# Weight split and convolution taps moved from GpSimd to VectorE in a two-block transformer kernel

## What is computed

```
h    = rms_norm(x) * w
proj = h @ w_in                        # 4128 columns, twice; 6176 columns once
# second block, of the projection's columns:
q,k,v (512 columns each)               # neighbourhood attention, with a norm over heads of 64
c    = short_conv(proj[..., 1024:2560])  # y[t] = w0*x[t-1] + w1*x[t] + w2*x[t+1], per channel
c    = silu(c); q,k parts: l2 norm over heads of 64, rotary embedding for the 1024 latent tokens
o    = gated delta rule over chunks of 64 tokens
```

## Time and profile before

| | |
|---|---|
| median of 3 runs | 4703.82 us (4698.98 to 4707.6) |
| the profiled execution, its own time | 4698.29 us |
| its span | 4696.4 us |
| PE busy | 3419.8 us, 73% |
| DVE busy | 2311.5 us, 49% |
| ACT busy | 1230.9 us, 26% |
| POOL busy | 860.2 us, 18% |
| granted TensorE clock, mean | 0.840 |

### The profile page before, as it was taken

The page is one execution under the profiler, slowest core; times in us unless marked ns, Lnnn a source line. Parts: engine busy times, 40 slices in busy tenths (PEclk is TensorE's granted clock), DMA queues, the critical chain, the costliest instruction groups (busy, mean ns, idle before and its releaser), DMA issues. The chain is left out here.

```text
span 4696.4 us, 75209 instructions
## 1 busy us (share of the span) xinstructions
PE 3419.8 (73%) x32108; PEld 2802.8 (60%) x32108; DVE 2311.5 (49%) x3831; ACT 1230.9 (26%) x2110; POOL 860.2 (18%) x724
## 2 busy tenths in 40 slices
PE   4997555567568995563767489977776779887688
PEld 4997454145238994453443279977765658776333
DVE  3111887377461116885766511056746844554333
ACT  2111332034231113330433211022234422221322
POOL 1221342110102122432001021132311012221100
PEclk9998656789779996655998689988887878999788
DMA  3222000540433221003013222155333121121411
GB/s 126 95 96 70 14 21 25 184 113 23 130 103 100 95 85 39 21 14 117 22 56 133 90 98 79 65 177 175 123 120 102 37 56 49 40 49 52 155 73 47
DMA packets 260142, 383.91 MB, mean 82 GB/s; under 512 B 46495, under 2 KB 192727, under 8 KB 258396
## 3 DMA queue, kind: packets, MB, share of 16 engines
q1 hardware_dynamic: 154618, 253.55, 17.2%
q10 hardware_dynamic: 105190, 125.55, 7.8%
HBM read 262.05 MB, written 123.13 MB: 82 GB/s over the span
## 5 line engine op out<-in xcount | busy, mean ns | idle before, releaser
L356 PE MATMUL psum<-proj_w_low,h_high 128*128 128x344 f32 (+1 forms) x2080 | 691.5, 332 | 55.0 <-POOL proj_w_low L341 55.0
L356 PE MATMUL psum<-proj_w_high,h_high 128*128 128x344 f32 (+1 forms) x2080 | 689.9, 332 | 0.0
L356 PE MATMUL psum<-proj_w_high,h_low 128*128 128x344 f32 (+1 forms) x2080 | 689.6, 332 | 0.0
L380 DVE COPY proj_y<-psum 128x344 f32<-128x344 f32 (+1 forms) x130 | 70.8, 545 | 964.8 <-PE psum L356 964.8
L356 PEld LDWEIGHTS psum<-proj_w_low,h_high 128*128 128x128 f32 x2080 | 392.0, 188 | 64.2 <-issue 56.1
L356 PEld LDWEIGHTS psum<-proj_w_high,h_high 128*128 128x128 f32 x2080 | 392.1, 188 | 8.1
L356 PEld LDWEIGHTS psum<-proj_w_high,h_low 128*128 128x128 f32 x2080 | 391.9, 188 | 8.2
L341 POOL TENSOR_TENSOR proj_w_low<-proj_raw,proj_cut 128x2752 fp32r<-128x2752 f32 (+1 forms) x31 | 203.0, 6549 | 1019.9 <-DVE proj_cut L371 1019.9
L403 ACT ACTIVATE proj_y<-psum 128x344 f32<-128x344 f32 (+1 forms) x130 | 61.9, 476 | 766.6 <-PE psum L356 766.6
L1256 PE MATMUL psum<-merge_wo,merge_yt 128*128 128x512 f32 x512 | 226.8, 601 | 13.5 <-ACT merge_yt L1201 10.0
L356 PE MATMUL psum<-proj_rest_w_low,h_high 128*128 128x304 f32 x640 | 199.5, 312 | 23.9 <-POOL proj_rest_w_low L341 23.2
(11 more groups left out here) (401 smaller groups left out, 7208.8 us busy)
## 6 DMA issues: line engine op xcount, KB each, us to landing
proj_raw<-in_w_in SPq DMA_DIRECT2D x24, 1376.0 KB, 6.8
proj<-proj_y ACTq DMA_DIRECT2D x192, 172.0 KB, 1.9
delta_x<-dn_qkv SPq DMA_DIRECT2D x40, 384.0 KB, 5.1
proj<-proj_y ACTq DMA_DIRECT2D x68, 224.0 KB, 1.9
dn_prep_x<-proj SPq DMA_DIRECT2D x54, 256.0 KB, 3.6
proj_raw<-in_w_in SPq DMA_DIRECT2D x7, 1792.0 KB, 7.4
norm_x<-x_stream SPq DMA_DIRECT2D x24, 512.0 KB, 3.3
modulate_w<-in_mod_w SPq DMA_DIRECT2D x6, 2048.0 KB, 9.0
```

What stands on the lines that cost most here:

```text
L356: last = PE.matmul(self.ps[:, j % 4, 0:self.width], hp[:, kt, tokens], wp[:, c % 2, kt, :], start=kt == 0 and n == 0, stop=kt == KT - 1 an ...
L380: V.tensor_copy(self.y[:, j % 4, :], self.ps[:, j % 4, 0:self.width]).then_inc(*self.copied[1].inc())
```

## The change

The low parts of the weights are written by DVE instead of POOL, right behind the cut. All three products of the convolution are on DVE, in one stream with the sums; the second sum moves from place 4u+2 to 4u+1, and ACT's first silu instructions from 4u+2.6 to 4u+1.6. Project gets `act_share`: with 1 the copies alternate as before, with 2 ACT makes them all; only `proj2_rest` gets 2. In NaPrepare, PE's transposes move from 3n+1.5 to 3n+2.2 and ACT's copy from 3n+2 to 3n+2.9. POOL keeps its other work in other stages.

```diff
@@ Project.__init__
-        self.high, self.low = self.event("act", "high", n_cols), self.event("pool", "low", n_cols)
+        self.high, self.low = self.event("act", "high", n_cols), self.event("dve", "low", n_cols)
         self.product = self.event("pe", "product", n)
-        self.copied = self.event("act", "copied0", n // 2), self.event("dve", "copied1", n // 2)
+        self.on_act = [j % 2 < act_share for j in range(n)]
+        self.copied = [self.event(e, f"copied_{e}", self.on_act.count(on)) for e, on in (("act", True), ("dve", False))]
@@ Project
-    def pool(self):
-        G = self.nc.gpsimd
-        for c in range(len(self.groups)):
-            yield self.start(c) + 2.7
-            G.wait_ge(*self.cutoff(c))
-            if c >= 2:
-                G.wait_ge(*self.product(self.first[c - 1] - 1))
-            G.tensor_tensor(self.wl[:, c % 2], self.raw[:], self.cut[:], ALU.subtract).then_inc(*self.low.inc())
+    def copy_of(self, j):
+        on = self.on_act[j]
+        return self.copied[0 if on else 1](self.on_act[:j].count(on))
@@ Project.pe
-                PE.wait_ge(*self.copied[j % 2](j // 2 - 2))
+                PE.wait_ge(*self.copy_of(j - 4))
@@ Project.dve_split
             V.tensor_scalar(self.cut[:].bitcast(U32), self.raw[:].bitcast(U32), HIGH, None, ALU.bitwise_and).then_inc(*self.cutoff.inc())
+            yield self.start(c) + 2.7
+            V.wait_ge(*self.cutoff(c))
+            if c >= 2:
+                V.wait_ge(*self.product(self.first[c - 1] - 1))
+            V.tensor_tensor(self.wl[:, c % 2], self.raw[:], self.cut[:], ALU.subtract).then_inc(*self.low.inc())
@@ Project.dve_copies
-        for j in range(1, self.items, 2):
+        for j in range(self.items):
+            if self.on_act[j]:
+                continue
@@ Project.act_copies
-        for j in range(0, self.items, 2):
+        for j in range(self.items):
+            if not self.on_act[j]:
+                continue
@@ NaPrepare.pe
-            yield 3 * n + 1.5
+            yield 3 * n + 2.2
@@ NaPrepare.act
-            yield 3 * n + 2
+            yield 3 * n + 2.9
@@ DeltaPrepare
-    def pool_unit(self, u):
-        G, s = self.nc.gpsimd, u % 2
-        yield 0
-        G.wait_ge(*self.loaded[s](self.loads[u]))
-        if u >= 2:
-            G.wait_ge(*self.done(u - 2))
-        G.tensor_tensor(self.tmp[:, s], *self.tap(u, 0), ALU.mult).then_inc(*self.tap0.inc())
-        yield 1.3
-        G.wait_ge(*self.tap_added(u))
-        G.tensor_tensor(self.tmp[:, s], *self.tap(u, 2), ALU.mult).then_inc(*self.tap2.inc())
@@ DeltaPrepare.dve_unit
-        c(V.tensor_tensor(y, *self.tap(u, 1), ALU.mult))
+        V.tensor_tensor(y, *self.tap(u, 1), ALU.mult)
+        c(V.tensor_tensor(tmp, *self.tap(u, 0), ALU.mult))
+        c(V.tensor_tensor(y, y, tmp, ALU.add))
         yield 1
-        V.wait_ge(*self.tap0(u))
-        V.tensor_tensor(y, y, tmp, ALU.add).then_inc(*self.tap_added.inc())
-        yield 2
-        V.wait_ge(*self.tap_added(u))
-        V.wait_ge(*self.tap2(u))
+        c(V.tensor_tensor(tmp, *self.tap(u, 2), ALU.mult))
         V.tensor_tensor(y, y, tmp, ALU.add).then_inc(*self.conv.inc())
@@ DeltaPrepare.act_unit
-        yield 2.6
+        yield 1.6
@@ build
-        rest = Project(k, "proj2_rest", above, h, [late] * 10, w2, 304, p2, 3136, row2)
+        rest = Project(k, "proj2_rest", above, h, [late] * 10, w2, 304, p2, 3136, row2, 2)
```

More of the change, by code:

```diff
@@ L301, with __init__ @@
 class Project(Stage):
-    def __init__(self, k, name, bottom, h_t, groups, w, width, dst, col0=0, row_of=lambda t: t * P):
+    def __init__(self, k, name, bottom, h_t, groups, w, width, dst, col0=0, row_of=lambda t: t * P, act_share=1):
         super().__init__(k, name, bottom)
@@ L408, in act_keeps @@
             yield j + 1.3
-            S.wait_ge(*self.copied[j % 2](j // 2))
+            S.wait_ge(*self.copy_of(j))
             row, first = self.row_of(t), self.col0 + c * self.width
@@ L1751, in __init__ @@
         self.stores = [sum(stores[u % 2:u + 1:2]) - 1 for u in range(n)]
-        self.tap0, self.tap2 = sig("pool", "tap0", n), sig("pool", "tap2", n)
-        self.tap_added, self.conv, self.logs = (sig("dve", x, n) for x in ("tap_added", "conv", "logs"))
+        self.conv, self.logs = (sig("dve", x, n) for x in ("conv", "logs"))
         self.logged, self.sigmoid = (sig("act", x, n) for x in ("logged", "sigmoid"))
@@ L1786, in tap @@
         return self.x[:, u % 2, d], self.w[:, d, self.C * part:self.C * part + self.C]
-    def pool(self):
-        self.nc.gpsimd.wait_ge(*self.consts(0))
-        yield from self.each(self.pool_unit)
-    def pool_unit(self, u):
-        G, s = self.nc.gpsimd, u % 2
-        yield 0
-        G.wait_ge(*self.loaded[s](self.loads[u]))
-        if u >= 2:
-            G.wait_ge(*self.done(u - 2))
-        G.tensor_tensor(self.tmp[:, s], *self.tap(u, 0), ALU.mult).then_inc(*self.tap0.inc())
-        yield 1.3
-        G.wait_ge(*self.tap_added(u))
-        G.tensor_tensor(self.tmp[:, s], *self.tap(u, 2), ALU.mult).then_inc(*self.tap2.inc())
     def dve(self):
```

## The result

Over 20 runs each on the same chip the kernel before took 4713.3 us (median) and the changed one 4687.6 us: ratio 0.9945, 95% interval 0.9929 to 0.996. That is 26 us less, between 19 and 33. The profiled execution of the changed kernel took 4685.6 us with a span of 4683.7, against 4698.3 and 4696.4 for the one that the earlier trace rows come from.

What follows compares the result with a forecast made beforehand. PE was taken to bound the lone projections, DVE the shared stage, a DVE-ACT-PE chain the attention stage. -12.2 - 32.1 - 5.1 + 0.9 = -48.5 took the median from 4703.8 to 4655.3 us; range 4622 to 4684.

Steps and rivals of the forecast that it cites:

- Term 1, the starts: Starts of all four projections: low parts on DVE at 1.07 ns an element bring the first matmuls sooner, -12.2 us.
- rival D: Low parts on DVE much slower than 1.07 ns an element, so starts gain nothing and shared stage loses 21; 4688, chance 0.03.
- Term 2, the shared stage: Shared stage: DVE's waits for POOL go, -32.1 us, and NaPrepare's later transposes give -5.1.
- I keep these whole: Shared stage: DVE's waits for a store and the rotation table, 57.4 us, stay unchanged; 64.5 idle in all.
- Rival A: PE becomes the bound of the shared stage and all 63.6 us of its wait go; 4622, chance 0.13.
- I allow 0 to +10: Shared stage: copies queued behind ACT's waits for DVE could hold PE a few us; counted as 0.
- The shift of NaPrepare's places: Shared stage: transposes 1.54 places later pay once, at the end, with fewer items left behind them, -5.1 us.
- signs of being wrong: PE newly waiting for ACT's copies, DVE's L1814 (now L1804) idle above 80 us, or PE never waiting for L1428.
- Term 3, the attention stage: Attention stage: added products +12.1, less waiting for POOL -2.0, stall gone -9.2; sum +0.9 us, between -12 and +14.
- DVE's busy share, 0.74: Attention stage: of 16.3 us of added products on DVE, 243.6/328 = 0.74, or 12.1 us, lies on the path.
- B: Freed time half refilled by longer waits at L1814, and the attention stage costs 14; change -14, 4690, chance 0.11.
- C: DVE saturates: +11.1 us in the shared stage, up to +16.3 in the attention stage; slower, 4719, chance 0.05.

Runs made afterwards that it cites:

- the runs with 230 and 207 us of DVE work: Changed kernel with the shared stage's copies alternating between ACT and DVE again (230, ratio 0.9949), and with DeltaPrepare's products back on POOL in that stage alone (207).

## Why the prediction was wrong

The sign was right and the size was not: 4655 was forecast with a range of 4622 to 4684, and 4687.6 was measured, 3.6 above the range; the change is -26 instead of -48.5. Of the 32 us between the two times 9.5 are the yardstick: the kernel before took 4713.3 in the median of 20 runs, not 4703.8 as in the three that the prediction had. The other 22.5 are the prediction's own.

**Term 1, the starts: right.** Forecast -12.2; measured -13.1 and -12.0 in the two profiles. The rate of 1.07 ns an element, on top of the small constant that the two given durations imply, held for the new shapes within 2% (2689 ns against 2.74 us), which also puts an end to rival D. The later groups cost nothing: DVE is busy 74.6 instead of 40.8 us in the first projection, and PE's busy time fills 359.6 of its 360.6.

**Term 2, the shared stage: nearly right in size, wrong in its form.** Forecast -37.2, measured -31.6 and -34.4. DVE's own work in the middle was forecast at 206.8 and came to 202.8; the stretched instructions are gone, all of them. The step that failed is "I keep these whole": the idle time was put at 64.5 and measured 77.6 (280.4 - 202.8), of it 70.9 before L1804. The forecast treated DVE's work plus fixed waits as the length. That came out to the microsecond for the low part alone (338.4), but not for the whole change: the runs with 230 and 207 us of DVE work and one length show it. Rival A had half of this: PE did come near to being the bound (291 of 324.9, clock 0.94 after 0.91), but kept 33.8 us of waits. They pass through engines that stand in order, PE for a copy, ACT for a result of DVE, DVE for a store or its own work. The text had put the copies queued on ACT at 0 in the sum ("I allow 0 to +10"); PE's waits for L409 are 21.9, but since they stay with the copies shared again, it is not the moved copies that were priced too low, it is the chain. The shift of NaPrepare's places was forecast at -5.1 as paid once; undoing it cost 7 to 10. Of the signs of being wrong that the prediction named, one came: the new wait for ACT's copies. L1804's idle time stayed below 80, and PE still waited for NaPrepare's input, though for 11.9 us where 20 to 35 were expected.

**Term 3, the attention stage: the failure.** Forecast +0.9 with ends -12 and +14; measured +14 against the mean of three traces with the old form of this stage (316.0 before, 330.0 with the low part alone, 323.1 with products back on POOL), and +21 to +25 against the one that the prediction was set against. Five more executions with the new form gave 335.6 to 338.5. Two steps of it failed:
- The move of ACT's silu from 2.6 to 1.6 was in the diff and in no term. It costs 6 to 15 us, 10.8 in the first pair of profiles, the largest part of the loss. The text says only that DVE is busier than ACT there, which is no reason to leave it out: ACT is busy 152 of 346 us, but in a step without DVE work it is the chain.
- The products were charged at DVE's busy share, 0.74. The doubled product cost its full length in every one of twelve steps. At full length the other terms come to 16.3 - 2.0 - 11.2 = +3.1. That the run with ACT's old place gives 326.2 - 323 = +3 as well is no proof, since the three traces behind the 323 lie 14 apart.

The stall behind POOL's table addition did go (11.17 us in that step), and nothing of it shows at the next unit, where 2 us were to be handed back. The wait of 11.8 us at a later unit is no part of that: it is 12.0 with the products on POOL.

**The sum redone with what was measured:** starts -12.6, shared stage -33, attention stage +14: -32, at the edge of the measured 19 to 33.

**The rivals.** B gave 4690, next to the measured time by luck: it stands on 4703.8 and a change of -14 where -26 was measured, with the right attention term (+14) and half the gain in the shared stage. D's 4688 is luck altogether. C is out too: nothing saturated to the point of a loss in the shared stage.

**The range** took +14 as the end of term 3 for the price of the products, and had nothing for the move of ACT. With 10.8 for it the forecast would have been 4666 and the upper end 4695. And the reference was one execution, whose attention stage of 316.0 was the shortest of three with that form; the clock in single steps, shown above, accounts for most of that.

What stays open: why the granted clock falls in some executions and not in others in the same steps, what the copies and products are worth singly without NaPrepare's new places, and how much of PE's waits in the shared stage hangs on the two buffers of `dn_prep_y`.

## What to carry to other kernels

Go through a diff for every changed place of an instruction, on engines with time to spare too: in a chain handed from engine to engine an instruction is hidden only in those steps where another engine is the longer one, so read its new neighbours step by step and not by busy shares. When an engine is relieved, ask which one sets the length next, and look first at in-order queues whose head waits for the relieved engine. Before a difference of some us between two profiles is put down to a change, compare the steps and the granted clock in them: the same stream took 316 and 330 us here. A change that helps one stage and hurts another is best split by stage. Low parts off POOL everywhere and products on POOL in the attention stage alone gave ratio 0.9924 after 0.9945, which the intervals do not tell apart; with that stage's large loads apart and the table additions later as well it was 0.9876, more than twice the gain.

## What the runs showed of the hardware that was not expected

The first thing is the clock in the attention stage, shown above: the same matmuls in the same step took 641 or 1138 ns, and the stage 316 or 330 us. The second is slighter. The matmuls of proj2, in the same program, ran at two spacings. Proj2 of the changed kernel in its two profiles, from the first to the last matmul (columns as above):

```profile
2719.10:3058.85 339.75, 339.75 (x1632) 308.17 (x1632) 55.59 (x45) 37.11 (x40) 0.00 (x0) 0.99 0.22 78
```
```profile
2716.30:3049.24 332.94, 330.56 (x1627) 306.38 (x1625) 56.19 (x46) 37.04 (x40) 0.00 (x0) 1.00 0.22 80
```

The median from one start to the next is 207 ns in the first and 203 in the second, all through the 68 items, with no wait in either, at a granted clock of 0.99 and 1.00. What sets them apart no run shows. Of the 14 profiles read here five show 207 and nine 203, and the changed kernel stands in both groups. It is worth 6.8 us, a quarter of this change's whole effect, so that stages that no edit touches have to be read beside those that it does. Delta, untouched as well, went from 546 to 575 us across the same profiles.
